# One VectorE remainder moved behind the second gated product at the end of six feed-forward stages

## What is computed

```
def swiglu(x, w13, w2):
    gate, up = jnp.split(x @ w13, 2, axis=-1)
    return (jax.nn.silu(gate) * up) @ w2
...
    for i in range(DEPTH):
        x = layer_norm(ALPHA * x + 0.5 * swiglu(x, ffn1_w13[i], ffn1_w2[i]), ln_g[i, 0], ln_b[i, 0])
        ...
        x = layer_norm(ALPHA * x + y, ln_g[i, 1], ln_b[i, 1])
        x = layer_norm(ALPHA * x + 0.5 * swiglu(x, ffn2_w13[i], ffn2_w2[i]), ln_g[i, 2], ln_b[i, 2])
```

## Time and profile before

| | |
|---|---|
| median of 3 runs | 2465.41 us (2463.21 to 2465.69) |
| the profiled execution | 2466.14 us |
| its span, first to last instruction | 2464.2 us |
| TensorE busy, matmuls | 2410.9 us, 98% of the span |
| VectorE busy | 1852.3 us, 75% |
| ScalarE busy | 1319.6 us, 54% |
| granted TensorE clock, mean | 0.996 of full speed |
| line 536, remainders of weight units | 370 instructions, 861.4 us |
| line 1769, remainders of gated chunks | 88 instructions, median 684 ns |

### The profile page before, as it was taken

How to read it: one execution, slowest core, us unless ns; L and a number is a source line. 1 busy time by engine, 2 the same in 40 slices (tenths; PEclk the granted TensorE clock), 3 DMA queues, 4 the chain that set the end, 5 groups by cost and what they waited for, 6 DMA issues and landing times. The chain is left out here.

```text
span 2464.2 us, 32871 instructions
## 1 busy us (share of the span) xinstructions
PE 2410.9 (98%) x13023; PEld 2027.1 (82%) x13023; DVE 1852.3 (75%) x2384; ACT 1319.6 (54%) x1637; POOL 409.4 (17%) x463
## 2 busy tenths in 40 slices
PE   9999999999999999999989999999999998999999
PEld 7888878888888888888878888888878876998998
DVE  5466679889875798898768888887675667897554
ACT  5444555555664556556556655664553355444442
POOL 0002310000001100000230000001359602580000
PEclk9999999999999999999999999999999999999999
DMA  8555445656554465565515565565445542336553
GB/s 273 188 187 156 143 146 190 204 171 200 193 172 137 137 197 196 177 199 188 167 58 184 188 209 171 187 206 158 133 149 191 189 153 71 116 124 205 171 188 111
DMA packets 313945, 418.10 MB, mean 170 GB/s; under 512 B 18761, under 2 KB 271042, under 8 KB 313794
## 3 DMA queue, kind: packets, MB, share of 16 engines
q1 hardware_dynamic: 313794, 416.01, 51.8%
HBM read 414.92 MB, written 1.05 MB: 169 GB/s over the span
## 5 line engine op out<-in xcount | busy, mean ns | idle before, releaser
L536 DVE TENSOR_TENSOR wlo<-raw,whi 128x2048 fp32r<-128x2048 f32 (+1 forms) x370 | 861.4, 2341 | 159.0 <-ACT whi L529 158.2
L529 ACT ACTIVATE whi<-raw 128x2048 fp32r<-128x2048 f32 (+1 forms) x375 | 700.4, 1887 | 6.0 <-DMA raw<-in_ffn_w_dram 3.1
L695 PE MATMUL ps<-whi,xh 128*128 128x512 f32 (+2 forms) x1367 | 510.8, 374 | 7.9 <-DVE wlo L1647 2.2
L697 PE MATMUL ps<-whi,xl 128*128 128x512 f32 (+2 forms) x1367 | 503.5, 368 | 0.0
L696 PE MATMUL ps<-wlo,xh 128*128 128x512 f32 (+2 forms) x1367 | 503.1, 368 | 0.0
L695 PE MATMUL ps<-whi,oh 128*128 128x512 f32 x944 | 380.1, 403 | 0.0
L697 PE MATMUL ps<-whi,ol 128*128 128x512 f32 x944 | 369.0, 391 | 0.0
L696 PE MATMUL ps<-wlo,oh 128*128 128x512 f32 x944 | 367.9, 390 | 0.0
L695 PEld LDWEIGHTS ps<-whi,xh 128*128 128x128 f32 x1367 | 258.0, 189 | 56.8 <-issue 11.9
L697 PEld LDWEIGHTS ps<-whi,xl 128*128 128x128 f32 x1367 | 257.9, 189 | 43.2
L696 PEld LDWEIGHTS ps<-wlo,xh 128*128 128x128 f32 x1367 | 258.2, 189 | 41.0
(11 more groups left out here) (412 smaller groups left out, 3988.8 us busy)
## 6 DMA issues: line engine op xcount, KB each, us to landing
raw<-in_ffn_w_dram SPq DMA_DIRECT2D x350, 512.0 KB, 4.9
raw<-in_ffn_w_dram SPq DMA_DIRECT2D x88, 1024.0 KB, 5.0
raw<-in_w_ff_dram SPq DMA_DIRECT2D x32, 1024.0 KB, 5.4
raw<-in_w_out_dram SPq DMA_DIRECT2D x20, 1024.0 KB, 4.9
raw<-in_w_in_dram SPq DMA_DIRECT2D x20, 1024.0 KB, 5.1
raw<-in_dsa_w_in_dram SPq DMA_DIRECT2D x32, 512.0 KB, 4.6
raw<-in_dsa_w_in_dram SPq DMA_DIRECT2D x12, 1024.0 KB, 5.1
raw<-in_fox_w_in_dram SPq DMA_DIRECT2D x16, 512.0 KB, 5.0
```

The lines of the kernel that those rows point to most:

```text
L529: act.activation(hi(u)[:, 0:w], raw[:, (slot[u] + 1) % SLOTS, 0:w], ACT.Copy).then_inc(sem("hi_ready"), n)
L536: dve.tensor_tensor(lo(u)[:, 0:w], raw[:, (slot[u] + 1) % SLOTS, 0:w], hi(u)[:, 0:w].bitcast(F32), ALU.subtract).then_inc(sem("lo_ready"), n)
L695: pe.matmul(o, ah, bh, start=start, stop=False, skip_group_check=True)
L697: return pe.matmul(o, al, bh, start=False, stop=stop, skip_group_check=True)
```

## The change

At the end of the last pair of a stage the first of the two splits is cut short by one unit: `split_lo` goes up to unit v + 6 and no longer to v + 7. The remainder of v + 7 is made by the later call, `split_lo(v + 8)`, which then issues two. So `gated_low(q + 1)` comes one remainder earlier in VectorE's list. The pairs at q = 3 and q = 6 are as before, and so are all the other engines' lists.

```
                         gate_rows(q + 1, 1, ps[:, 5, 256:512])
                         gated_low(q)
-                        split_lo(dve, v + 7)
+                        split_lo(dve, v + 6 if q + 1 == FIT - 1 else v + 7)
                         gated_low(q + 1)
                         split_lo(dve, v + 8)
```

## The result

The changed kernel takes 2468.86 us (median of 20 runs, 2467.56 to 2471.08), the one before 2465.47 us (median of 20, 2462.60 to 2466.20): 3.4 us more. The ratio is 1.0016, with a 95% interval from 1.0009 to 1.0023, that is 2.2 to 5.7 us slower. The profiled execution took 2468.32 us, its span 2466.4.

The account below looks back on a forecast made before the run. VectorE's list was taken as the path at six places, up to `xn`; its idle time, 4 x 0.53 + 0.56 + 0.52 = 3.2 us, on the 2465.41 us median gave 2468.6 us, range 2464.0 to 2470.8.

Parts of the forecast that it names:

- What ends last: Before line 2352 VectorE's chain to `xn` ends last, 0.02 us ahead; TensorE's six `xn` waits (1.6 us) also taken as ground.
- TensorE's gain at `ol`: At line 2537 the wait for `ol` goes; TensorE is 1.03 us ahead at line 695, turned into longer waiting at line 2352.
- VectorE's loss: VectorE idles ahead of the moved `ol` until `oh` is ready: 0.53 us at the first place, delaying statistics and `xn`.
- the stage without pairs: Stage used for the ScalarE-to-VectorE hand-over: `oh` ends at 190.35, `ol` starts at 190.38, 0.03 us.
- The sum: VectorE's idle time over the six places: 4 x 0.53 + 0.56 + 0.52 = 3.2 us slower.
- The size of the restart: A VectorE wait also costs the 0.07 us overlap of successive remainders; without that, 0.46 us a place, 2.8 us in sum.
- Costed at nothing: v + 7's remainder, 1.1 us later, has 8 us of cover before line 733; v + 8's input and ring slots also cost nothing.
- TensorE's wait decides: Rival: statistics wait for TensorE, not VectorE's list, so early `ol` gains 1.03 to 1.21 us a place; 2458.7 us, chance 0.08.
- The delay was not absorbed: Rival claimed VectorE's 0.53 us vanishes after the turning where another chain ends last: no change, 2465.4 us, chance 0.12.
- The granted clock: Rival: TensorE's longer gap at the turning lowers its clock, at least 1.6 us a place more; 2478 us, chance 0.04.
- the row with 1.65 us: An idle time elsewhere on TensorE that left the granted clock at 1.00; the expected 1.5 us gap lies below it.
- stretches far from the six places change: One of the prediction's own signs of being wrong, looked for in the profile after the change; no size given.

Follow-up runs that it names:

- quarter: The change, but with a quarter of the moved v + 7 remainder kept ahead of the last `ol`, against the kernel before: 2465.32 us beside 2465.35, ratio 1.0001.
- parts_early: Kernel before with the last `ol` ahead of v + 7's remainder and v + 8's remainder in three pieces inside the norm: 2458.62 us, ratio 0.9975.
- v8_early: Kernel before with the last `ol` moved as in the change and v + 8's remainder made inside the norm, behind the first `xl`: 2461.04 us, ratio 0.9982.
- earliest: Kernel before with the last `ol` two remainders earlier, ahead of v + 6 as well: 2481.89 us beside 2464.97, ratio 1.0070.

## Why the prediction was right

*What ends last.* Right, but one of its two grounds was misread. The six waits for `xn` of 1.6 us in the earlier trace rows are not at the six places: five stand at tile 1 of norms behind the first stage and behind mixers, the sixth at the last norm of the program. At the places the matmuls of before show no bracket. The first of the six, and then what does show it at the first place, TensorE's weight load:

```profile
205.87 1.09 PE L2352 MATMUL ps<-ident,xn 128*128 128x128 f32 x8 [0.23 <-ACT xn L1005]
519.40 0.86 PEld L2352 LDWEIGHTS ps<-ident,xn 128*128 128x128 f32 x8 [0.39 <-ACT xn L1005]
```

The other ground holds: `xn` ends 0.02 us ahead of line 2352, before and in the change. quarter and parts_early show it from both sides: without VectorE's idle time nothing is lost and nothing won, and once VectorE's list is out of the way the early `ol` is worth 1.1 us a place.

*TensorE's gain at `ol`.* 1.03 us forecast, 1.02 measured at the first place. It all went into the wait at line 2352, 1.56 us by the bracket where 1.5 was forecast. The list of waits has 12 of them there and not six, since the six old ones elsewhere stay.

*VectorE's loss.* `ol` at 511.51 forecast, 511.53 measured, with the whole trace 0.02 later; the statistics at 516.53 forecast, 516.54 measured. The hand-over of 0.03 us from the stage without pairs held.

*The sum.* 3.2 us forecast, 3.17 in the steps, 3.4 in the medians with 2.2 to 5.7 as interval. The second place is the largest with 0.58 us, as was said (0.56), the fourth with 0.54 isn't the smallest; such differences of 0.02 us are below what two profiles can tell.

*The size of the restart.* If VectorE had no overlap to lose, the step would have been 0.46 us. The measured ones are 0.47 to 0.58, mean 0.53, and the overlap stands in the rows of the change again: the second pair of remainders takes 4.48 us, the statistics start 4.40 us behind its start. The prediction set this against the Trainium skill (page "VectorE: DVE Perf Modes", section "The DRAIN you can't avoid"), but that section also says that a next operation that is not held back starts earlier. Read with this sentence, the section does not exclude the overlap of 0.07 us that the rows show; so the trace speaks against the 0.46 us and not against the section.

*Costed at nothing.* The late remainder of v + 7 cost nothing; the quarter kernel has it nearly as late and is as fast as before.

*The rivals.* That TensorE's wait decides fell in the kernel as it is, and its condition was the right one: it holds in v8_early and parts_early, where VectorE's work ahead of the statistics is 2.2 us shorter; 1.06 us a place is within its price of 1.03 to 1.21. The advice of the Trainium skill (page "Perfetto Trace Analysis", section "Optimization Strategy") to find what blocks the busiest engine leads astray here if only the longest wait is looked at, and holds once the wait behind it is counted too. The delay was not absorbed. The granted clock did not fall at the places; it is 1.00 in the 5 us round line 2352 at all six, as here at the first:

```profile
518.00:523.00 5.00, 3.44 (x20) 1.00 0.59 210
```

The ground given for this, that the gap lies below the row with 1.65 us, proves less than it seemed. In earliest a wait of 2.22 us left the clock at 1.00 at three places and was followed by 0.50 to 0.54 at the other three, and in parts_early it fell round a wait of 0.80 us in the attention. One profile of the change shows no fall at the places; that it could not happen is not shown.

*What I had wrong.* "I am wrong if stretches far from the six places change": they do, by up to 2 us from one profile to the next, in kernels of either kind. It was no usable test; the steps at the places were.

## What to carry to other kernels

Removing a wait of the busiest engine brings nothing if what this engine needs next comes from a chain that runs on regardless; look at the next wait, however small (0.12 us between starts here), and ask whose chain ended it. Moving an operation ahead in the list of the engine that carries that chain cost here the time that its input was late (0.53 us a place), even though the operation itself was finished earlier. First take work that nobody needs yet out of that chain (here one remainder, in pieces, into gaps that existed); then the early operation paid. Before a dose experiment is read as proof, look at the clock behind the waits that it makes.

## What the runs showed of the hardware

A remainder cut into pieces costs little: 512 columns start 0.60 us ahead of the next instruction (511.41 to 512.01) and 1536 columns 1.67 (512.61 to 514.28), together 2.27 us against 2.21 for the whole, 0.06 us for the cut. I had taken 0.1.

The granted clock is not settled by the length of one wait. Six waits of 2.22 us in one profile (earliest) were followed by 1.00 three times and by 0.50 to 0.54 three times. In the latent attention it fell in two of nine profiles, to 0.58 over 8 us in parts_early, round a wait of 0.80 us that in before is 0.84 us long and left it at 1.00.
